# First norm in token layout, projections from the start, two convolution blocks on POOL, and a later first triangular transpose

## The reference

```
a    = rmsnorm(x, norm_mix)                    # over 1024 channels
proj = a @ w_in                                # q,k,v (3072), z, beta, a, glu (1024), gates (2048)
qkv  = silu(causal_conv4(qkv)); q,k = l2norm(q,k)
g    = -exp(a_log) * softplus(a + dt_bias); beta = sigmoid(beta)
o, S = gated delta rule, 8 heads of 128x128, in chunks (triangular inverse, then states)
cv   = silu(layernorm(causal_conv31(u) + b)),  u = glu product, 512 channels
x   += (g_a * (o*silu(z) @ w_gdn_out) + g_b * (cv @ w_conf_out)) @ w_out
x   += moe(rmsnorm(x))                         # top 4 of 32 experts, clamped SwiGLU, 402 MB of weights
x   += (p @ w_ple_proj) * sigmoid(rmsnorm(x) @ w_ple_gate);  y = rmsnorm(x)
```

## Time and profile before

| | |
|---|---|
| Median of 3 runs | 1551.79 us (1551.20 to 1554.34) |
| The profiled execution | 1548.72 us, span 1547.0 us |
| TensorE busy | 1400.1 us (91% of the span) |
| VectorE busy | 502.9 us (33%) |
| ScalarE busy | 256.7 us (17%) |
| POOL busy | 49.6 us (3%) |
| DMA | 462.7 MB, 299 GB/s over the span |
| TensorE's granted clock | 0.98 of full |

### The profile page before, as it was taken

How to read it: one execution, slowest core, us unless ns; L and a number is a source line. 1 busy time by engine, 2 the same in 40 slices (tenths; PEclk the granted TensorE clock), 3 DMA queues, 4 the chain that set the end, 5 groups by cost and what they waited for, 6 DMA issues and landing times.

```text
span 1547.0 us, 19781 instructions
## 1 busy us (share of the span) xinstructions
PE 1400.1 (91%) x7416; PEld 810.2 (52%) x7416; DVE 502.9 (33%) x1086; ACT 256.7 (17%) x518; POOL 49.6 (3%) x71
## 2 busy tenths in 40 slices
PE   3899989898999999989989889889889899999987
PEld 3587777676788843443433434424424434444346
DVE  1366677778522450211211202202202102112124
ACT  2351322414230310100100000001001001100023
POOL 2010011101000000000000000000000000000000
PEclk9899989999999999999999999999999999999999
DMA  7142322324239679999999999999999999999950
GB/s 190 35 129 69 97 87 85 110 75 120 69 106 352 206 298 421 421 422 422 422 422 422 420 421 422 422 422 422 422 421 421 421 422 422 421 422 421 421 217 29
DMA packets 120464, 462.72 MB, mean 299 GB/s; under 512 B 9795, under 2 KB 68692, under 8 KB 71140
## 3 DMA queue, kind: packets, MB, share of 16 engines
q1 hardware_dynamic: 100924, 449.05, 72.4%
q10 hardware_dynamic: 19472, 12.74, 2.9%
HBM read 455.75 MB, written 6.68 MB: 299 GB/s over the span
## 4 chain that ended last, share of the span: by engine, by line
PE 64%; DMA 20%; DVE 9%; issue 2%; ACT 2%; ACTq 1%; SPq 0%; POOL 0%; DVEq 0%; POOLq 0%
DMA ring<-in_w_gate_up 20%; PE bank L1025 15%; PE bank L983 13%; PE bank L814 9%; PE bank L941 6%; PE bank L1046 4%; PE bank L858 3%; PE bank L686 2%; PE bank L892 2%; PE bank L1097 2%; DVE lent L1671 2%; PE bank L976 1%; ACTq L1149 1%; PE bank L692 1%; PE bank L1005 1%
## 5 line engine op out<-in xcount | busy, mean ns | idle before, releaser
L983 PE MATMUL bank<-ring,lent 128*64 128x512 f32 (+1 forms) x2304 | 459.1, 595 | 66.4 <-DMA ring<-in_w_gate_up 66.2
L983 PEld LDWEIGHTS bank<-ring,lent 128*64 128x64 f32 (+1 forms) x2304 | 148.0, 131 | 361.8 <-issue 342.9
L814 PE MATMUL bank<-lent,ring 128*128 128x264 f32 x896 | 234.0, 406 | 2.9 <-DVE big L1692 1.6
L1025 PE MATMUL bank<-ring,lent 128*64 128x512 f32 (+1 forms) x1152 | 226.7, 595 | 0.2 <-ACT lent L1421 0.2
L814 PEld LDWEIGHTS bank<-lent,ring 128*128 128x128 f32 x896 | 170.2, 200 | 37.0 <-issue 7.5
L1841 DVE TENSOR_SCALAR big<-bank 128x512 f32<-128x512 f32 x32 | 20.6, 686 | 431.4 <-PE bank L983 431.3
L1025 PEld LDWEIGHTS bank<-ring,lent 128*64 128x64 f32 (+1 forms) x1152 | 69.8, 131 | 135.8 <-issue 128.7
L1415 ACT ACTIVATE big<-big 128x512 f32<-128x512 f32 x32 | 19.6, 630 | 511.9 <-DVE big L1841 511.9
L941 PEld LDWEIGHTS bank<-st,big 88*128 88x128 f32 x768 | 87.0, 192 | 12.8 <-issue 11.4
L941 PE MATMUL bank<-st,big 88*128 88x128 f32 x768 | 90.0, 277 | 0.6 <-ACT outputs L1412 0.5
L1859 DVE TENSOR_TENSOR xT<-xT,bank 128x264 f32<-128x264 f32 x128 | 54.9, 429 | 96.8 <-PE bank L1046 95.3
(11 more groups left out here) (354 smaller groups left out, 1119.5 us busy)
## 6 DMA issues: line engine op xcount, KB each, us to landing
ring<-in_w_gate_up SPq DMA_DIRECT2D x256, 1024.0 KB, 19.1
ring<-in_w_down SPq DMA_DIRECT2D x128, 1024.0 KB, 23.5
ring<-in_w_in SPq DMA_DIRECT2D x28, 1024.0 KB, 5.2
st<-in_state_gdn ACTq DMA_DIRECT2D x8, 512.0 KB, 4.3
out<-st ACTq DMA_DIRECT2D x8, 512.0 KB, 3.3
ring<-in_w_gdn_out SPq DMA_DIRECT2D x4, 1024.0 KB, 5.1
ring<-in_w_out SPq DMA_DIRECT2D x4, 1024.0 KB, 9.7
ring<-in_w_ple_gate SPq DMA_DIRECT2D x4, 1024.0 KB, 15.8
```

What stands on the lines that cost most here:

```text
L814: last = mm(b[:, 0:T], w[:, k, o:o + P], aT[:, k, :], start=k == 0, stop=k == KD - 1)
L983: last = mm(bank[t][lo:hi, :], x_slots[:, c, lo:hi], w, start=False, stop=c == KD - 1)
L1025: last = mm(bank[4 + t][lo:hi, :], hT[:, m, lo:hi], w, start=m == 0, stop=m == KD - 1)
```

## The change

- The first norm is computed with tokens on the partitions: ScalarE and VectorE square x as loaded and sum along the row, the scaled rows (`xn`, laid in ring slots that are free) are transposed, and the gain is applied as the banks are drained into `aT`. The gain comes by a DMA of its own. TensorE runs 16 products of ones before. The product by ones (`rms1`) goes.
- The projections begin as soon as `aT` is there. Parameter, x, history and per-layer transposes, beta and a (one product of 40 rows in place of two of 8) and the decay's chain are now `early` entries in the timetable, after thirds of blocks 0 to 6.
- The small loads move from ScalarE's queue to SP's, between chunks 0, 1, 2 and 6 of `w_in`.
- Two of the four blocks of the long convolution go to POOL, one tap for each third of blocks 21 to 41, as a product and a sum. VectorE does the other two, two taps a block in blocks 14 to 47, and the sample parts of all four.
- In `GDN_PLAN` an empty third comes ahead of `t1`, and the one ahead of `osq` goes.

```diff
-GDN_PLAN = [..., ["scores"], ["tokens"], ["t1"],
+GDN_PLAN = [..., ["scores"], ["tokens"], [], ["t1"],
...
-            ["vn0"], ["s1"], ["ks", "store1"], ["vn1"], ["s2", "o"], [], ["osq"], ["onorm"], ["oexp"], ["ofin"]]
+            ["vn0"], ["s1"], ["ks", "store1"], ["vn1"], ["s2", "o"], ["osq"], ["onorm"], ["oexp"], ["ofin"]]
...
-TAPS = {n: [1, 1, 1] for n in range(14, 40)}
-TAPS.update({14: [0, 0, 2], 15: [2, 2, 2], 16: [2, 1, 1], 17: [2, 1, 2], 18: [2, 1, 1], 19: [2, 1, 1]})
-TAPS.update({n: [2, 2, 2] for n in range(40, CONF_END)})
+TAPS = {n: [1, 0, 1] for n in range(14, CONF_END)}
+POOL_TAPS = range(21, 42)
+EARLY = {(0, 0): ["par1"], (0, 1): ["par2", "par0"], (1, 0): ["ba"], (1, 2): ["hist0"], (2, 0): ["sp"], (2, 1): ["hist1"],
+         (2, 2): ["ln"], (3, 0): ["x00", "x01"], (3, 1): ["gT"], (3, 2): ["gbt"], (4, 0): ["x10", "x11"], (4, 1): ["gct"],
+         (4, 2): ["esc"], (5, 0): ["x20", "x21"], (5, 1): ["ch0"], (5, 2): ["ch1"], (6, 0): ["pT"], (6, 1): ["pTs"]}
+DVE_BLOCKS = 2
...
+            between = {0: load_params, 1: load_rows, 2: load_rest, 6: copy_states}
...
+            for t, name, n in ((0, "xn_act", 1), (1, "xn_dve", 1), (2, "xn_dve", 2)):
+                pe.wait_ge(s[name], n)
                 for h in range(2):
...
+                    x_transposes(f"xn{t}{h}", xn, t, h)
...
+                elif name == "ba":
+                    pe.wait_ge(s["ba_loaded"], 16 * 2)
+                    pe.wait_ge(s["consts"], CONSTS)
+                    b = to_fill(pe, name)
+                    for k in range(KD):
+                        last = mm(b[0:32 + H, 0:T], wba[:, k, :], aT[:, k, :], start=k == 0, stop=k == KD - 1)
+                    fill_done(name, last)
...
+            act.wait_ge(s["x_loaded"], 16 * 3)
+            tell(A(x_sq[0], xs[:, 0, :], ACT.Square, accum_out=x_sum[:, 0:1]))
+            tell(A(x_rstd[:, 0:1], x_sum[:, 0:1], ACT.Sqrt, bias=eps[:, 0:1], scale=1.0 / D), "xroot")
+            tell(A(x_sq[0][0:TS], xs[0:TS, 2, :], ACT.Square, accum_out=x_sum[0:TS, 2:3]))
+            tell(A(x_rstd[0:TS, 2:3], x_sum[0:TS, 2:3], ACT.Sqrt, bias=eps[0:TS, 0:1], scale=1.0 / D), "xroot")
+            act.wait_ge(s["squares"], 1)
+            tell(A(x_rstd[:, 1:2], x_sum[:, 1:2], ACT.Sqrt, bias=eps[:, 0:1], scale=1.0 / D), "xroot")
+            act.wait_ge(s["rstd_ready"], 1)
+            A(xn[:, 0, :], xs[:, 0, :], ACT.Copy, scale=x_rstd[:, 0:1]).then_inc(s["xn_act"], 1)
...
+                elif name == "sp":
+                    act.wait_ge(s["params_loaded"], 16 * PARAM_DMAS)
+                    tell(A(small8[:, 2:3], small8[:, 0:1], ACT.Exp), "expa")
+                    act.wait_ge(s["sp_in"], 1)
+                    tell(A(tmp8b, tmp8b, ACT.Exp), "e1_ready")
+                elif name == "ln":
+                    act.wait_ge(s["gates_in"], 1)
+                    tell(A(tmp8b, tmp8b, ACT.Ln), "ln_ready")
...
+            def conf_tap(at):
+
+                i, tap = divmod(at, CK)
+                i += DVE_BLOCKS
+                x, w = cv[:, i, 0:TP], wdw[:, tap, i:i + 1].broadcast_to([P, TP])
+                if tap == 0:
...
+                else:
+                    tell(g_.tensor_tensor(pool_tap[:], up[:, i, tap:tap + TP], w, ALU.mult))
+                    tell(g_.tensor_tensor(x, x, pool_tap[:], ALU.add), "conf_done" if at == CK * (CB - DVE_BLOCKS) - 1 else None)
```

More of the change, by code:

```diff
@@ L143, in _timetable @@
             out.append(("block", n, third))
+            out += [("early", name, 0) for name in EARLY.get((n, third), [])]
             for g, start in enumerate(GDN_STARTS):
@@ L155, in _timetable @@
                 out.append(("conf_tap", n, third))
+            if n in POOL_TAPS:
+                out.append(("pool_tap", n, third))
     return out
@@ L245, in build @@
         ps_tok = carve(upper, at + 3072, 3, PLE)
-        stage = carve(upper, at + 3072 + 768, 3, P)
+        stage = carve(upper, at + 3072 + 768, 4, P)
+        xn = carve(lent_slots, 0, 3, D)
+        x_sq = [carve(lent_slots, (3 + i) * D, D) for i in range(2)]
         big = sbuf("big", [P, 3 * KD * T])
@@ L378, in plan @@
             count[b] += 1
-        early = ["par0", "par1", "par2"] + [f"x{t}{h}" for t in range(3) for h in range(2)]
-        early += ["rms1", "hist0", "hist1", "ch0", "ch1", "pT", "pTs", "beta", "a", "gbt", "gct", "gcf"]
+        early = ["gain"] + [f"xn{t}{h}" for t in range(3) for h in range(2)]
+        for names in EARLY.values():
+            for name in names:
+                early += {"gct": ["gct", "gcf"], "sp": [], "ln": [], "gT": [], "esc": []}.get(name, [name])
         for i, n in enumerate(early):
@@ L665, in _ @@
-            pe.wait_ge(s["gT_ready"], 1)
-            wait_drained(pe, "beta")
-            b = to_fill(pe, "gbt")
-            for i, src in enumerate((gT, gT, betaT, betaT)):
-                last = tr(b[:, i * H:(i + 1) * H], chunk(src, i % 2), ident[0:H, 0:H])
-            fill_done("gbt", last)
-            wait_drained(pe, "gbt")
-            b = to_fill(pe, "gct")
-            for i in range(4):
-                last = mm(b[:, i * H:(i + 1) * H], (causal if i < 2 else ones)[:], gbt[:, i % 2, :], start=True, stop=True)
@@ L813, in _ @@
                     for k in ((0, 1, 2), (3, 4, 5), (6, 7))[x]:
+                        if n == 0 and k % 4 == 0:
+                            for t in range(3):
+                                wait_drained(pe, f"xn{t}{k // 4}")
                         last = mm(b[:, 0:T], w[:, k, o:o + P], aT[:, k, :], start=k == 0, stop=k == KD - 1)
@@ L1335, in _ @@
                         out_of(A(dst[:, i, :], b[:, 0:T], ACT.Sigmoid), name)
+                elif kind == "early":
+                    early_step(n)
                 elif kind == "gdn":
```

436 lines of the change are left out of this document (259 added, 177 removed).

## The result

The changed kernel takes 1541.8 us (1541.3 to 1545.2) against 1554.3 (1551.2 to 1556.1) for the kernel before, five runs of each on one chip: a ratio of 0.9927 [0.991, 0.9945], which is 11 us (the ratio is that of the means; the medians lie 12.5 us apart). That of before (1548.72) is faster than all five of these runs, so sums over the two traces come out some 4 us smaller than the 11 us of the runs.

What follows compares the result with a forecast made beforehand. TensorE's arrival at the end of the projections sets the end, the experts' DMA-bound length being fixed. Terms -24 (start), -2, +12, -6 give -20: 1548.72 to 1529, plus 3.1 for the median, 1532 us; range 1522 to 1541, wide 1511 to 1548.

Steps and rivals of the forecast that it cites:

- the wide one: Whole kernel: 1511 to 1548 us, from just under the covered-contention case to beyond the stalled one, without the slow case.
- its own signs of being wrong: Experts starting less than 10 or more than 35 us earlier, or VectorE's exposed operations keeping their length beside POOL.
- Part 1: The start: first projection at 17.5 us, 41.3 earlier; 14 of work and 3 of stall come back, gain 24 us.
- early steps stall: Rival, first blocks: ScalarE's tables and back and forth with VectorE stall them the full 14 us; 1542 us, chance 0.15.
- Part 3: Two convolution blocks to POOL: VectorE is relieved but waits beside POOL's operations; blocks 21 to 41 get 12 us longer.
- 39 was the term: Blocks 21 to 41: VectorE's added waits beside POOL, 138 operations x 0.62 meeting POOL x 0.45 us.
- The rival by which each exposed operation costs 1.2 us: "POOL holds the port", blocks 21 to 41: VectorE and POOL take turns, stretch grows 56 us; 1575 us, chance 0.09.
- The term of +12 in blocks 21 to 41: Blocks 21 to 41 take 12 us longer, half of VectorE's net 24 us reaching TensorE; bounds -7 and +56.
- that of -2 in blocks 14 to 20: Blocks 14 to 20: VectorE does 14 taps in place of 28, 2 us gained, bounds 0 and 4.
- that of -6 behind: Behind blocks 21 to 41, in 355 to 400 us: 6 us back from TensorE's gaps, the T1 share included.
- Part 2: Triangular steps a third later: T1 waits shrink 1.4 us each, 4.2 in all; squares cost 0 to 1.4 a group.
- T1's 2.8 and the 1 for the squares: Blocks 21 to 41: T1's gain of 2.8 us and the squares' cost of 1, set against each other.

Runs made afterwards that it cites:

- S1: Changed kernel with all four convolution blocks back on VectorE and the recurrence in the old order, so the early start alone: 1523.4 us, 0.9815 of the kernel before.
- E3: Changed kernel with `t1` and the squares of the outputs back at their old thirds; early start and POOL's taps stay: 1523.7 us, 0.9809 of the kernel before.
- E1: Changed kernel with POOL's taps left out, its two channel blocks filled with zeros once (part of the computation missing): 1517.5 us, 0.9769 of the kernel before.
- S4: Changed kernel with the old order of the recurrence and POOL's taps left out (part of the computation missing): 1509.0 us, 0.9714 of the kernel before.
- E4: Kernel before with only the two convolution blocks moved to POOL, start and recurrence order as before: 1549.9 us, 0.9963 of the kernel before.
- S2: Changed kernel with `ad`'s drain ahead of the short convolution in VectorE's order, in a block's second third: 1524.8 us, 0.9816 of the kernel before.
- F3: F1 with POOL's product taking the weight as a scalar for each partition, not a broadcast tensor: 1512.0 us, 0.9733 of the kernel before.
- S3: Changed kernel with `t1` a whole block later than before, not a third; the squares keep their empty third: 1531.2 us, 0.9865 of the kernel before.
- F1: E3 with the drains of `ad`, `dm` and `lt` ahead of the short convolution in a block's second third: 1521.0 us, 0.9796 of the kernel before.

## Why the prediction held, and the step of it that failed

The forecast was 1532 us; 1541.8 lies 0.8 us above its own range of 1522 to 1541 and inside the wide one, on the faster side. Of the 20 us that it forecast, 11 came. One of its own signs of being wrong is met: the experts were to start at least 10 us earlier, and in the two profiled executions their first product comes at 540.4 us in place of 547.6, 7.2 us earlier. The sum was right in sign and half right in its terms.

**Part 1, right.** The first projection came at 18.05 us for 17.5, 40.8 us earlier for 41.3. What came back in the first seven blocks is 17.0 us (40.8 to 23.8), which the prediction had as 14 of TensorE's work and 3 of stall; the one gap of over 1 us there, 2.38 us, is the stall. Alone it is worth 29 us by the runs (S1) and 22.9 by S1's profiled execution against that of before; the two differ by the place of that execution among its runs and by what a run varies. The "early steps stall" rival fell, though its time of 1542 is the one measured, and that is chance: the stretch in which it would have lost the time ran without a gap of over 2.4 us.

**Part 3, right in the mechanism, too dear in sum.** POOL's operations took 0.66 and 0.79 us for 0.7. VectorE's work there came to 133.9 us (E3: 132.5) for 151: it was made 112 by the relief, as E1's 110.1 shows, and contention added 21 us (E3 against S4's 111.8) to 24 (the kernel after against E1), where 39 was the term. 138 exposed operations times 0.62 was not far off: 27 of 36 short-convolution taps and 28 of 39 long ones ran beside POOL. It is the wait that was too long, 0.3 us (0.78 against 0.485) for 0.45. The rival by which each exposed operation costs 1.2 us fell with it. The term of +12 in blocks 21 to 41 measures +10.2 (E4), that of -2 in blocks 14 to 20 measures -6.6, and that of -6 behind measures -6.3. So POOL's taps were put at +4 and alone give -6 (0.9963, or -4 by the medians).

The Trainium skill, page GPSIMD Engine Reference, section Key points, says that GpSimd shares its interfaces to the buffer with VectorE and collides with VectorE operations that have two inputs there. The trace agrees with the kind of operation: 0.682 us against 0.488 for taps, 0.692 and 0.691 for drains from a bank. A copy with one input in the buffer is held as well: L1657, 128x16, took 1.23 us beside POOL in all of its four places, and its twin L1658, which begins before POOL's next operation, 0.18. So the prediction's split, by which operations with two inputs in the buffer are the exposed ones, was not complete.

**Part 2, the step that failed.** The prediction said of the later `t1`: "1.4 us each, 4.2 us in all, if VectorE is no later than before". VectorE was no later for `t1`, and that wait did go: 9.3 to 2.4 us. What was missed is that an empty third ahead of `t1` doesn't delay `t1` alone. It moves every step behind it, the fifteen steps of the ladder in each group, by a third against the blocks, and a block's thirds are not alike: in the second one of a q/k/v block VectorE's product and two taps of the short convolution stand ahead of whatever step is entered there. All four groups start at the same third, and a level of the ladder is three thirds long, so it is always the same step that meets them. In the old plan that was `dm`, whose drain cost 6.5 us of waits (E3, L1685), and `ad` came in the first third (5.4 us of waits in the kernel before, 4.1 in E3). In the new one it is `ad`: 23.4 us, in gaps of up to 3.8 us, and with them the granted clock falls, to 0.90 in blocks 21 to 41 from 0.97 in S2. In the old plan the sample steps stood ahead of `ad` and the convolution ahead of `dm`; in the new one both stand ahead of `ad`. That this is why `ad` pays more in this place than `dm` did is read from the two timelines, and not tried apart. So a term that the sum had left at about nothing measured +18 (E3 against the kernel after), and S2 shows the cause: with the drain ahead of the convolution in VectorE's list, 17 of the 18 us are back. The trade "with T1's 2.8 and the 1 for the squares set against each other and the rest in the clock" had looked only at the two steps that the diff names.

The total came out near only because errors of opposite sign met. By the ratios, step by step: the start -29 for -24 (S1), POOL's taps on top of it -1 for +4 (S1 to E3), the plan +18 for about nothing (E3 to the kernel after). These steps lead from the one kernel to the other, so that they add up to the measured -11 says nothing by itself; -20 was forecast. Had the first two terms been right as forecast, the 18 us of the plan would have brought 1532 to 1550, outside the wide range: that the time fell within it is luck. "Contention" as the reason why the long blocks took 194 us in place of 178 would have been a plausible story, since VectorE has POOL beside it at the longest of those gaps. It holds for the size of the gaps (16.2 us without POOL's taps, 23.4 with) and not for their number, and six of the fourteen, 6.6 us, lie outside the blocks in which POOL has taps.

What stays open: why POOL's form with one tensor doesn't hold VectorE; whether F3's product would give as much under the new plan; and what in S3 makes the long waits of blocks 30 to 34.

## What to carry to other kernels

When a step of a woven schedule is moved, everything behind it moves too: write down for each of these steps what then stands ahead of it in the order of every engine, and do it for one whole period, before the gain of the step itself is worked out. Where TensorE waits for a drain that stands behind work with time to spare, try the exchange: it gave 17 us under the new plan (S2), and nothing under the old one, where the wait only moved from one drain to the other (F1). In a bundle, take each edit alone: here the smallest one lost 18 of the 29 us that the early start had gained.

## What was not expected of the hardware

A POOL product of 128x256 by a scalar per partition takes 0.975 us and one by a broadcast tensor 0.681, so the form with one tensor is the slower, by 43%. Yet it is the one that hardly disturbs VectorE: a tap that begins under it takes 0.48 to 0.67 us, and one that begins under the two-tensor form ends 0.28 us after POOL does, whatever is left of POOL's operation, in all 17 cases of F1. So what a POOL operation takes and what it costs VectorE are two prices. These are times of the profile, and the reason for either is not shown.

TensorE's gaps can cost more again in the clock: from S2 to the kernel after, idle time in blocks 21 to 41 grew by 6.4 us and busy time for the same work by 10.1, at 0.97 and 0.90 granted; from E3 it is 9.1 and 9.7. It is no fixed price: F1 is idle for 22.4 us in these blocks, less than E3's 23.5, and busy for 156.9 at 0.93, against 151.9 at 0.96.
